# Branch layers of a fused six-layer stack: attention in steps between weight slabs, branch products behind their gates, one half of a depthwise convolution on GpSimd

## The reference

```python
h = _rmsnorm(x, mix_norm[l])
z = h @ w_in[l]
(c_a, c_b, s_b, s_c, s_x, a_q, a_k, a_v, f_q, f_k, f_v, f_f, z_gate) = jnp.split(z, SPLITS, axis=-1)
u = c_a * jax.nn.sigmoid(c_b)
u = _causal_depthwise_conv(u, conf_dw[l]) + conf_dw_b[l]          # 31 taps, 256 channels
u = jax.nn.silu(_layernorm(u, conf_ln_g[l], conf_ln_b[l]))
p_conf = u @ conf_w_out[l]
p_sc = (s_b * _causal_depthwise_conv(s_c * s_x, sc_conv[l])) @ sc_w_out[l]     # 3 taps
...
p_swa = _sliding_window_attention(q, k, v, swa_sink[l], rel_bias) @ swa_w_o[l] # 4 heads of 64
...
p_fox = _forgetting_attention(q2, k2, v2, log_f) @ fox_w_o[l]                  # 4 heads of 64
g = jax.nn.sigmoid(z_gate).reshape(bsz, t, N_BRANCH, D_MODEL)                  # four gates of width 1024
merged = (g[:, :, 0] * p_conf + g[:, :, 1] * p_sc + g[:, :, 2] * p_swa + g[:, :, 3] * p_fox)
x = x + merged @ w_out[l]
```

## Time and profile before

| | |
|---|---|
| time, median of 3 runs (lowest to highest) | 3695.88 us (3694.83 to 3697.13) |
| the profiled execution: its time, its span | 3692.8 us, 3691.0 us |
| mean granted TensorE clock | 0.968 |
| TensorE matmul busy | 3516.1 us (95%) |
| VectorE busy | 2498.2 us (68%) |
| ScalarE busy | 1506.0 us (41%) |
| GpSimd busy | 40.3 us (1%) |
| DMA | 593 MB, 161 GB/s, 44.8% of the 16 engines |

### The profile page before, as it was taken

How to read it: one execution, slowest core, us unless ns; L and a number is a source line. 1 busy time by engine, 2 the same in 40 slices (tenths; PEclk the granted TensorE clock), 3 DMA queues, 4 the chain that set the end, 5 groups by cost and what they waited for, 6 DMA issues and landing times.

```text
span 3691.0 us, 66144 instructions
## 1 busy us (share of the span) xinstructions
PE 3516.1 (95%) x27769; PEld 3382.5 (92%) x27769; DVE 2498.2 (68%) x2828; ACT 1506.0 (41%) x1494; POOL 40.3 (1%) x22
## 2 busy tenths in 40 slices
PE   8999999998999997899999999999978999998899
PEld 8998899996899996599999899999968999997799
DVE  7668677665667667566767866766857676676666
ACT  4363334343434343443436333434343343434333
POOL 0000030000000000000000000000000000000000
PEclk9999999998999998899999999999989999998899
DMA  6543475543355552055554335555423545543254
GB/s 245 183 171 121 126 211 192 182 171 114 112 185 182 182 182 103 12 186 182 183 187 162 115 126 182 183 183 192 163 101 133 186 171 193 182 172 137 80 190 163
DMA packets 98920, 593.00 MB, mean 161 GB/s; under 512 B 25684, under 2 KB 26836, under 8 KB 27736
## 3 DMA queue, kind: packets, MB, share of 16 engines
q1 hardware_dynamic: 97280, 586.71, 44.8%
q10 hardware_dynamic: 1496, 4.20, 0.3%
HBM read 588.77 MB, written 2.11 MB: 160 GB/s over the span
## 4 chain that ended last, share of the span: by engine, by line
PE 82%; DVE 9%; ACT 4%; issue 4%; DMA 1%; SPq 0%; DVEq 0%; ACTq 0%
PE prod L417 19%; PE prod L418 18%; PE prod L419 18%; PE acc L417 7%; PE acc L418 7%; PE acc L419 7%; ACT high L974 3%; DVE low L1317 2%; PE acc L604 2%; DVE work L1600 1%; DVE work L1871 1%; PE stat L615 1%; PE prod L623 1%; DMA work<-start 0%; PE acc L675 0%
## 5 line engine op out<-in xcount | busy, mean ns | idle before, releaser
L417 PE MATMUL prod<-xh,high 128*128 128x256 f32 x5968 | 1703.7, 285 | 45.6 <-DVE gs L1934 13.3
L418 PE MATMUL prod<-xl,high 128*128 128x256 f32 x5968 | 1689.7, 283 | 0.0
L419 PE MATMUL prod<-xh,low 128*128 128x256 f32 x5968 | 1689.3, 283 | 0.0
L1317 DVE TENSOR_TENSOR low<-raw,high 128x2048 fp32r<-128x2048 f32 x537 | 1237.8, 2305 | 607.9 <-ACT high L974 604.5
L974 ACT ACTIVATE high<-raw 128x2048 fp32r<-128x2048 f32 x550 | 1047.9, 1908 | 914.2 <-PE prod L419 459.4
L417 PEld LDWEIGHTS prod<-xh,high 128*128 128x128 f32 x5968 | 1134.4, 190 | 66.3 <-issue 27.2
L418 PEld LDWEIGHTS prod<-xl,high 128*128 128x128 f32 x5968 | 1134.4, 190 | 0.9
L419 PEld LDWEIGHTS prod<-xh,low 128*128 128x128 f32 x5968 | 1134.0, 190 | 0.0
L417 PE MATMUL acc<-ends,high 128*128 128x256 f32 x2112 | 594.8, 282 | 0.0
L419 PE MATMUL acc<-ends,low 128*128 128x256 f32 x2112 | 594.4, 281 | 0.0
L418 PE MATMUL acc<-ends,high 128*128 128x256 f32 x2112 | 594.3, 281 | 0.0
(11 more groups left out here) (198 smaller groups left out, 2619.1 us busy)
## 6 DMA issues: line engine op xcount, KB each, us to landing
raw<-stream SPq DMA_DIRECT2D x550, 1024.0 KB, 4.8
work<-rpb SPq DMA_DIRECT2D x16, 256.0 KB, 6.4
work<-bias_shifted ACTq DMA_DIRECT2D x2, 1024.0 KB, 4.8
cst<-consts SPq DMA_DIRECT2D x1, 1416.0 KB, 12.0
x<-x_in SPq DMA_DIRECT2D x1, 1024.0 KB, 4.8
raw<-stream SPq DMA_DIRECT2D x2, 512.0 KB, 6.9
work<-bias_by_distance ACTq DMA_DIRECT2D x2, 512.0 KB, 4.6
bias_shifted<-work ACTq DMA_DIRECT2D x1, 1024.0 KB, 6.0
```

Source lines behind the costliest of these rows:

```text
L417: nc.tensor.matmul(out, wh, ah, start=start, stop=False, **kw)
L418: nc.tensor.matmul(out, wh, al, start=False, stop=False, **kw)
L419: return nc.tensor.matmul(out, wl, ah, start=False, stop=stop, **kw)
L1317: v.tensor_tensor(low[:, s % LOW, :], raw[:, s % RAW, :], high[:, s % HIGH, :].bitcast(F32), ALU.subtract).then_inc(low_ready, 1)
```

## The change

Only the branch layers change, in seven respects.

1. TensorE's list: the attention is cut into `scores`, `turn` (transposes) and `outputs` for each pair of heads, and these are placed between the slabs 8 and 19. Transposes go to `acc` banks, not to `prod`.
2. The order of the slabs: the gates of the short convolution's branch come first (12 to 15) and its product is slab 16; then the gates of the two attention branches (17 to 24) and their products (25, 26); then the gates of the long convolution (27 to 30) and its product (31). `br_g` has room for three gates instead of four.
3. VectorE's list: `largest` and `shares` of a pair stand between its slabs. `shares` only makes the reciprocal; the probabilities are scaled on ScalarE (`scaled_shares`).
4. The taps of the long convolution are for one chunk of channels only, 128 of 256; they come behind `lows`, up to three a slab, up to slab 27.
5. GpSimd does the other chunk: one `tensor_scalar`, then 30 times a `tensor_scalar` into `br_tap` and a `tensor_tensor` add, each waiting for the one before. It starts when the low part of slab 11 is made; TensorE waits for `conv_ready` before the layer norm's statistics.
6. The layer norm lies between slabs 27 and 29 and its result is multiplied behind slab 30.
7. The merged sum is split in four pairs of chunks: ScalarE copies the high part, VectorE subtracts for the low one.

The host's packing of the weight stream follows the new order. The new lists, cut to their order:

```diff
@@ TensorE, branches @@
-                for j in range(5 + 12):
-                    project(s + 7 + j)
-                pe.wait_ge(mix_ready, c.up(mix_ready))
-                stats([(ones, br_conv[:, i, :]) for i in range(2)])
...
-                attention("branches", SWA_HEADS + FOX_HEADS, br_scores, br_values)
...
+                project(s + 7)
+                project(s + 8)
+                scores(0, 2)
+                project(s + 9)
+                project(s + 10)
+                scores(1, 4)
+                turn(0)
+                project(s + 11)
+                project(s + 12)
+                outputs(0)
+                scores(2, 5)
+                turn(1)
+                project(s + 13)
+                project(s + 14)
+                outputs(1)
+                scores(3, 5)
+                turn(2)
+                project(s + 15)
+                pe.wait_ge(mix_ready, c.up(mix_ready))
+                branch(s + 16, 2)
+                outputs(2)
+                turn(3)
+                project(s + 17)
+                project(s + 18)
+                outputs(3)
+                for j in range(19, 25):
+                    project(s + j)
+                for br in range(2):
+                    pe.wait_ge(ot_ready, ot_base + 2 * br + 2)
+                    branch(s + 25 + br, br)
+                project(s + 27)
+                pe.wait_ge(mix_ready, c.up(mix_ready))
+                pe.wait_ge(conv_ready, c.up(conv_ready))
+                stats([(ones, br_conv[:, i, :]) for i in range(2)])
+                project(s + 28)
+                pe.wait_ge(sq_ready, c.up(sq_ready))
+                stats([(ones, br_sq[:, i, :]) for i in range(2)])
+                project(s + 29)
+                project(s + 30)
+                pe.wait_ge(mix_ready, c.up(mix_ready))
+                branch(s + 31, 3)
@@ ScalarE, branches @@
-                ahead(s + 7, 5)
-                for j in range(16):
-                    sigmoid(br_g[:, 2 * j:2 * j + 2, :], (gs, hid)[j % 2][:, :, :])
-                    ahead(s + 12 + j)
...
+                ahead(s + 7, 2)
...
+                exponents(0)
+                ahead(s + 9)
+                scaled_shares(0)
+                ahead(s + 10)
+                turned(0)
+                exponents(1)
+                ahead(s + 11)
+                scaled_shares(1)
+                gate(0)
+                ahead(s + 12)
+                turned(1)
+                output_high(0)
+                exponents(2)
+                gate(1)
+                ahead(s + 13)
+                scaled_shares(2)
+                gate(2)
+                ahead(s + 14)
+                turned(2)
+                output_high(1)
+                exponents(3)
+                gate(3)
+                ahead(s + 15)
+                scaled_shares(3)
+                ahead(s + 16)
+                turned(3)
+                output_high(2)
+                gate(4)
+                ahead(s + 17)
+                gate(5)
+                ahead(s + 18)
+                output_high(3)
+                for g in range(6, 12):
+                    gate(g)
+                    ahead(s + 13 + g)
+                ahead(s + 25, 2)
+                gate(12)
+                ahead(s + 27)
...
+                for j in range(4):
+                    pair = slice(2 * j, 2 * j + 2)
+                    act.wait_ge(merged, c.up(merged))
+                    nc.scalar.activation(oh[:, pair, :], br_m[:, pair, :], ACT.Copy).then_inc(ot_high, 1)
+                    if j == 2:
+                        ahead(s + 31)
@@ VectorE, branches @@
-                for j in range(11):
-                    gate(j)
-                    for k in range(4 * j, min(4 * j + 4, CONV_K)):
-                        tap(br_conv, br_u, lambda i, k: par(f"dw{l}", i * CONV_K + k), k, lambda i: par(f"dwb{l}", i))
-                    if 8 <= j < 8 + SC_K:
-                        tap(br_sc, br_t, lambda i, k: par(f"sc{l}", i * SC_K + k), j - 8)
-                    lows(s + 12 + j)
...
+                lows(s + 8)
+                largest(0)
+                scaled(hid[:, :, :], product(s + 9)[:, :, :])
...
+                lows(s + 9)
+                shares(0)
+                taps(1)
...
+                lows(s + 10)
+                largest(1)
+                scaled(br_sb, product(s + 11)[:, :, :])
+                lows(s + 11)
+                shares(1)
+                taps(2)
...
+                gate(s + 12, 0)
+                lows(s + 12)
+                largest(2)
+                gate(s + 13, 1)
+                lows(s + 13)
+                shares(2)
+                low_out(0)
+                for k in range(SC_K):
+                    link(tap(br_sc, br_t, lambda i, k: par(f"sc{l}", i * SC_K + k), k))
+                gate(s + 14, 2)
+                lows(s + 14)
+                link(v.tensor_tensor(br_sc, br_sc, br_sb, ALU.mult))
+                split(br_sc, 4, 2, mix_ready, (oh, ol))
+                largest(3)
+                gate(s + 15, 3)
+                lows(s + 15)
+                shares(3)
+                low_out(1)
+                taps(1)
+                branch(s + 16, 0, 4, first=True)
+                lows(s + 16)
+                gate(s + 17, 4)
+                lows(s + 17)
+                low_out(2)
+                taps(3)
...
+                for g in range(7, 12):
+                    gate(s + 13 + g, g)
+                    lows(s + 13 + g)
+                    taps(3)
+                for br in range(2):
+                    branch(s + 25 + br, 1 + br, 8 + 4 * br)
+                    lows(s + 25 + br)
+                gate(s + 27, 12)
+                lows(s + 27)
+                taps(3)
...
@@ GpSimd @@
+            for l in range(LAYERS_2):
+                s = STAGES[LAYERS_1 + l][1]
+                pool.wait_ge(low_ready, s + 8 + LOW + 1)
+                out = br_conv[:, 1, :]
+                nc.gpsimd.tensor_scalar(out, br_u[:, 1, 0:T], par(f"dw{l}", CONV_K), par(f"dwb{l}", 1), ALU.mult, ALU.add).then_inc(pool_step, 1)
+                steps += 1
+                for k in range(1, CONV_K):
+                    nc.gpsimd.tensor_scalar(br_tap, br_u[:, 1, k:k + T], par(f"dw{l}", CONV_K + k), None, ALU.mult).then_inc(pool_step, 1)
+                    steps += 1
+                    pool.wait_ge(pool_step, steps)
+                    ins = nc.gpsimd.tensor_tensor(out, out, br_tap, ALU.add)
...
```

More of the change, by code:

```diff
@@ L236, in build @@
         exp_done = sem("exp_done")
+        share_ready = sem("share_ready")
         p_ready = sem("p_ready")
@@ L1038, in ffn, with attention @@
                 ahead(s0 + FFN_SLABS - 1)
-            def attention(heads, kind, sink=None):
-                out = xh if kind == "branches" else oh
+            def attention(heads, kind):
                 probs, probsT = buffers[kind]
@@ L1500, in ffn, with attention @@
                     low_part(KC - 1, gain)
-            def attention(heads, kind, scale=None, bias=None, sink=None, between=None):
-                out = (xh, xl) if kind == "branches" else (oh, ol)
+            def attention(heads, kind, scale=None, bias=None):
                 probs, _ = buffers[kind]
@@ new lines, in shares, with tap @@
+                def shares(i):
+                    for h in (2 * i, 2 * i + 1):
+                        st = small[:, h % 4, :]
+                        dve.wait_ge(exp_done, c.up(exp_done))
+                        if h < SWA_HEADS:
+                            link(v.tensor_tensor(st[:, 2:4], st[:, 2:4], st[:, 4:6], ALU.add))
+                        v.reciprocal(st[:, 6:8], st[:, 2:4]).then_inc(share_ready, 1)
+                def tap(out, src, w, k, first_bias=None, chunks=2):
+                    for i in range(chunks):
@@ L1881, in branches, with taps @@
-                own(v.tensor_tensor(br_sc, br_sc, br_sb, ALU.mult), mix_ready)
-                gate(11)
+                    return last
+                taps_done = [0]
+                def taps(n):
+                    for k in range(taps_done[0], taps_done[0] + n):
+                        last = tap(br_conv, br_u, lambda i, k: par(f"dw{l}", i * CONV_K + k), k, lambda i: par(f"dwb{l}", i), 1)
+                        if k < CONV_K - 1:
+                            link(last)
+                        else:
+                            own(last, mix_ready)
+                    taps_done[0] += n
@@ new lines, in branches, with gate, branch @@
+                c.up(sig_ready, 16)
+                def gate(s, g):
+                    if g >= 2:
+                        dve.wait_ge(sig_ready, sigmoids + g - 1)
+                    scaled((gs, hid)[g % 2][:, :, :], product(s)[:, :, :])
+                def branch(s, at, gates, first=False, last=False):
+                    dve.wait_ge(sig_ready, sigmoids + gates)
+                    for j in range(4):
+                        b = product(None if j < 3 else s)
```

(18 more changed lines are left out.)

240 lines of the change are left out of this document (139 added, 101 removed).

## The result

| | before | after |
|---|---|---|
| median (lowest to highest), 10 runs of each | 3696.53 us (3694.83 to 3700.49) | 3705.02 us (3702.53 to 3709.30) |
| ratio, 95% interval | | 1.0022 [1.0014, 1.0030] |
| span of the profiled execution | 3691.0 us | 3701.9 us |
| first branch layer, gate of slab 7 to the first read of slab 32 | 213.9 us | 220.3 us |
| second branch layer, the same | 217.4 us | 220.0 us |

The account below looks back on a forecast made before the run. VectorE and ScalarE in turn were taken to bound the branch layers, with TensorE waiting. The steps summed to 222.7 us against 217.4, +5.3 a layer, +10.6 in all: 3695.9 + 10.6 = 3706.5 us, range 3676 to 3736.

Parts of the forecast that it names:

- (a): Slabs 7 to 12: VectorE's added attention work, waits and collisions make 39.8 us, against 28.5 before.
- (b): Gates 12 to 15, last two attention pairs, short convolution and slab 16: work 28.6, collisions 4.1, waits 21.7, sum 54.4 us.
- (c): Slabs 17 to 24: eight turns of 6.87 us and two low outputs, 55.7 us.
- (d): Branch products 25 and 26 and gate 27: 20.9 us, with the loop of branch products unchanged.
- (e): Gate 27 to gate 28, with the last three taps ahead of the statistics: 15.7 us.
- Here the order decides: Slabs 17 to 24: taps behind the low part leave the 2.6 us wait open, 6.87 us a turn against 6.59 before.
- collision term: GpSimd's work slows VectorE's instructions beside it: 7 us a layer, nearly all on VectorE's path; bounds 0 and 17 or more.
- TensorE waits, and pays for each wait again with slow matmuls: Branch stages before the change: VectorE and ScalarE set the pace; TensorE, 31 us idle, restarts at the 1.2 GHz level.
- ScalarE's term: ScalarE carries 12 us more, including four table loads; only what stands before a high part costs.
- TensorE's queue swallows the waits: Rival, chance 0.22: half the 28 us of waits in (a) and (b) vanish into score matmuls, 3678 us.
- Collisions nothing: Rival, chance 0.22: GpSimd's work beside VectorE costs nothing, 7 us less, -1.7 a layer, 3692 us.
- hoped-for 50 us a layer: Gain per branch layer if nothing but TensorE's whole work, 165 us, counted.

Follow-up runs that it names:

- e9_no_four_row: e8 without the forgetting heads' 4-row score products (32 matmuls a layer left out, so it computes something else): 3645.0 us, ratio 0.9861.
- e1_taps_in_wait: Changed kernel with the three taps of slabs 17 to 24 and 27 between gate and low part, not behind the low part: 3675.3 us, ratio 0.9943.
- e8: Changed kernel, taps between gate and low part, slab 16 read before slab 18's low part, high part before sigmoid in slabs 12-15 and 17-24: 3661.7 us.
- e11: e8 with gate 15's sigmoid before the high part, and slab 34's high and low part behind the merged sum's split: 3648.9 us, ratio 0.9875.
- e6: e1_taps_in_wait with GpSimd's half of the long convolution back on VectorE as pairs of taps: 3675.5 us, ratio 0.9944.
- e10: e8 with GpSimd's half of the long convolution back on VectorE as pairs of taps: 3667.3 us, ratio 0.9924.
- e12: e11 with GpSimd's half of the long convolution back on VectorE as pairs of taps: 3653.7 us, ratio 0.9886.
- e4_before_gpsimd_half: Kernel before with one part of the change alone, GpSimd doing half the channels of the long convolution: 3694.9 us, ratio 0.9993.

## Where the prediction was right and where it was wrong

Step by step, us of the first layer from TensorE's end of slab 7 (2595.45) to the first read of slab 32 (2819.32):

| step | forecast | measured |
|---|---|---|
| (a) to gate 12 | 39.8 | 39.0 |
| (b) to gate 17 | 54.4 | 55.5 |
| (c) to branch 25 | 55.7 | 57.1 |
| (d) to gate 27 | 20.9 | 20.4 |
| (e) to gate 28 | 15.7 | 15.6 |
| gates 28 to 30 | 13.4 | 12.9 |
| last branch, slab 32 | 22.8 | 23.4 |
| sum | 222.7 | 223.9 |

**Right, and shown.** "Here the order decides" holds: the turn of step (c) was called from the order of three calls, and exchanging two of them gave 29.7 us. (Before had eight tap instructions a turn against three, 2.4 times their time and not "twice".) The wait in slab 16 was where it was put; TensorE's wait there is 4.5 us in the first layer and 6.6 in the second, where 7 was forecast. The wait of 2.60 before each low part of (c), and gates about every 6.9 us (7.05), came as written. GpSimd was done by 2675, earlier than the 2690 allowed.

**Right by two errors that cancel.** The collision term was mis-sized: 7 us a layer forecast, 4.8 by the excess of VectorE's own instructions, and 0.5 to 2.1 us by the run that takes them away. It was charged as if VectorE were last everywhere. In (b) it is not: VectorE's own work with collisions is 30.7 us there instead of 32.7, and its waits are 24.8 instead of 21.7. Of these the ones for high parts are 1.9 us shorter than forecast; 4.1 us are waits for TensorE at gates 13 and 15, of which the forecast has none:

```profile
2645.73 0.69 DVE L1552 TENSOR_TENSOR newt<-prod,rstd 128x512 f32<-128x512 f32 x1 [1.65 <-PE prod L425]
...
2669.16 0.69 DVE L1552 TENSOR_TENSOR newt<-prod,rstd 128x512 f32<-128x512 f32 x1 [2.41 <-PE prod L425]
```

What filled the place of the missing collisions was thus TensorE, which runs at half clock in or right behind the forgetting heads' scores, without a pause (busy by stretch, around the two pairs):

```profile
2637.00:2641.00 4.00, 4.00 (x22) 3.69 (x21) 2.12 (x1) 3.98 (x5) 3.73 (x4) 0.62 0.00 0
...
2657.00:2661.00 4.00, 4.00 (x13) 2.88 (x13) 1.81 (x1) 2.11 (x3) 3.73 (x4) 0.50 0.00 0
```

The step "TensorE waits, and pays for each wait again with slow matmuls" knows one cause of a low clock, the pause; e9_no_four_row shows a second, in which there is none. It was tried in the mended order only; that it is a cause of the 0.63 in the earlier trace rows and of the rows just shown is argued from the same products standing there. My 20 us for the attention's matmuls took the full clock throughout. The other term that was off is the turn of (c), 1.4 us: three single taps take 1.52 us, 0.51 each, where I took 0.457 from pairs. With collisions at their measured price and nothing else put right, the forecast would have been 3693 to 3697, 8 to 12 us too low: that the time came out within 1.5 us is luck, though the direction and the steps are not. ScalarE's term was short as well: it has six more table loads a layer, not four, and carries 16 us more, not 12.

**Not foreseen.** The layer of before that I used is the shorter one by this measure: 213.9 against 217.4 us. After is 220.3 and 220.0. So the step is 6.4 in one layer and 2.6 in the other, where the forecast took 5.3 twice: 1.1 too little and 2.7 too much, which again offset each other. Of the 3.5 us by which the old second layer is longer, 1.5 lie before gate 12, 0.6 at the statistics and 1.4 behind the last gate; their cause was not followed up.

**The rivals.** "TensorE's queue swallows the waits" was given 0.22 and a time of 3678; its deciding point, gates in (c) at 5.7 us, was not met in the changed kernel. It is met in e1_taps_in_wait, which came out at 3675.3, but that nearness to 3678 is chance: there the gain comes from the taps' place in (c), not from waits swallowed in (a) and (b). "Collisions nothing" was nearer on its own term, 0.5 to 2.1 us a layer, and wrong in the sum: with GpSimd idle the time is 3704.2, not 3692. Where the hoped-for 50 us a layer went is thus named by about half. The changed first layer is 59 us above the 165 of TensorE's own work (223.9 less 165). Orders take back 14 in slabs 17 to 27 by the taps' place, 7 at slab 16, and 8 more by the other edits of e8 and e11, the sigmoids of slabs 12 to 15 and the ends (e11_orders_and_ends is 28.9 us a layer below after). The 4-row products' own 8.6 us are in the 165 already; only what the low clock adds to them and behind them belongs to the rest. That rest, some 30 us, has in it the waits before the branches and the slow restarts behind them, and no run took it apart.

The Trainium skill, GPSIMD Engine Reference, section Elementwise, gives 1.03 cycles an element for one input and 2.6 for two, by which the multiplication should be the shorter of the two. Here it is the longer: the one-input multiplication with a scalar per partition takes 0.93 us undisturbed, the two-input add 0.73, both 128x256. The first operation of each layer, one input too, took 0.56, so the form alone does not explain the 0.93; no run here varies the columns. Its section Engine selection, which advises VectorE for such work, fits the pair e1 and e6 (no gain) and not quite the pairs e8 and e10, e11 and e12 (5 us).

## What to carry to other kernels

Work taken off an engine can be worth nothing while a wait for the other engine of the chain stays open next to it: write out one turn of each engine as gate, wait, low, taps, and put the free work into the wait before moving it elsewhere. Summing the stretched instructions of an engine overstates a collision wherever another engine is last; a run without the neighbour's work prices it. When an order is changed, look at what each call is next needed for: a low part for two slabs ahead stood twice before something that TensorE was waiting for.

## What the runs showed of the hardware

- TensorE's granted clock fell from 1.00 to 0.50 while it was busy without pause, in score products with operands of 4 rows (e8_all_orders), and stayed at 1.00 with those left out (e9_no_four_row).
- GpSimd at 128x256, float32, undisturbed: multiplication by a scalar per partition 0.93 us, add of two tensors 0.73; beside a low part of VectorE, itself 2.29 us, the add took 2.72 (the first row of the fence for e4_before_gpsimd_half; 2.76 at most there) and the multiplication up to 3.03:

```profile
2608.16 0.93 POOL L2227 TENSOR_SCALAR work<-work,prm 128x256 f32<-128x256 f32 x1
2609.17 0.73 POOL L2230 TENSOR_TENSOR work<-work 128x256 f32<-128x256 f32 x1
```

- Small VectorE operations of two SBUF operands suffer most in proportion: in e8_all_orders one of 2 elements a partition took 0.68 us beside GpSimd, and the next 0.16.

```profile
2630.07 0.68 DVE L2005 TENSOR_TENSOR small<-small 128x2 f32<-128x2 f32 x1
...
2630.86 0.16 DVE L2005 TENSOR_TENSOR small<-small 128x2 f32<-128x2 f32 x1
```
